# Attention with keys on the partitions: maxima from one product, exponents not transposed, the causal mask as a product

## What is computed

```python
sc = einsum('bgpqd,bgnd->bgpqn', qb, k_cmp)            # compressed keys
p_c = softmax(where(valid_c, sc, NEG_INF)); o_c = p_c @ v_cmp
ss = einsum('bgpqd,bgqnld->bgpqnl', qb, k_sel)         # selected blocks
p_s = softmax(where(key_pos <= t_pos, ss, NEG_INF)); o_s = p_s @ v_sel
sw = einsum('bgpqd,bgkd->bgpqk', qb, kwb)              # window
p_w = softmax(where(valid_w, sw, NEG_INF)); o_w = p_w @ vwb
o = gate0 * o_c + gate1 * o_s + gate2 * o_w
```

## Time and profile before

| | us |
|---|---|
| median of 3 runs (lowest to highest) | 2381.58 (2381.36 to 2381.64) |
| the profiled execution | 2382.09 |
| its span | 2380.3 |
| PE busy in it | 2370.0 |
| DVE busy | 1332.7 |
| ACT busy | 899.4 |
| POOL busy | 310.5 |

### The profile page before, as it was taken

The page is one execution under the profiler, slowest core; times in us unless marked ns, Lnnn a source line. Parts: engine busy times, 40 slices in busy tenths (PEclk is TensorE's granted clock), DMA queues, the critical chain, the costliest instruction groups (busy, mean ns, idle before and its releaser), DMA issues.

```text
span 2380.3 us, 33586 instructions
## 1 busy us (share of the span) xinstructions
PE 2370.0 (100%) x11768; PEld 2002.1 (84%) x11768; DVE 1332.7 (56%) x2199; ACT 899.4 (38%) x1376; POOL 310.5 (13%) x305
## 2 busy tenths in 40 slices
PE   9999999999999999999999999999999999999998
PEld 7899988888888888888888888888889998888887
DVE  8667765344465764443586644446756676534444
ACT  6267833222233432222233322223426773322223
POOL 2211140000040120000033000003420114000003
PEclk9999999999999999999999999999999999999999
DMA  4710023232233232322233223233370002223232
GB/s 165 224 46 2 2 69 108 88 101 93 99 105 106 89 106 91 103 97 97 97 99 106 97 91 104 89 106 105 121 208 27 2 2 89 97 89 106 89 105 89
DMA packets 64616, 220.58 MB, mean 93 GB/s; under 512 B 7680, under 2 KB 7808, under 8 KB 64512
## 3 DMA queue, kind: packets, MB, share of 16 engines
q1 hardware_dynamic: 58320, 208.59, 26.3%
q0 software_dynamic: 5184, 8.40, 1.6%
q10 hardware_dynamic: 1008, 2.21, 0.3%
HBM read 208.68 MB, written 2.10 MB: 89 GB/s over the span
## 4 chain that ended last, share of the span: by engine, by line
PE 99%; DVE 0%; DMA 0%; ACT 0%; SPq 0%; issue 0%; DVEq 0%
PE bank L1516 95%; PE bank L1796 3%; DMA x<-x_in 0%; PE bank L1826 0%; DVE branch L1281 0%; DVE big L1509 0%; SPq L434 0%; DVE rden L1276 0%; ACT L588 0%; DVE w_lo L939 0%; DVE rden L1278 0%; ACT w_hi L572 0%; PE bank L1700 0%; ACT xs_hi L581 0%; ACT xg L907 0%
## 5 line engine op out<-in xcount | busy, mean ns | idle before, releaser
L1516 PE MATMUL bank<-xs_hi,w_hi 128*128 128x512 f32 (+1 forms) x1808 | 708.9, 392 | 1.1 <-DVE xs_lo L947 0.5
L1516 PE MATMUL bank<-xs_lo,w_hi 128*128 128x512 f32 (+1 forms) x1808 | 703.3, 389 | 0.0
L1516 PE MATMUL bank<-xs_hi,w_lo 128*128 128x512 f32 x1792 | 697.3, 389 | 0.0
L939 DVE TENSOR_TENSOR w_lo<-raw,w_hi 128x1024 fp32r<-128x1024 f32 x369 | 469.7, 1276 | 230.7 <-ACT w_hi L572 226.3
L572 ACT ACTIVATE w_hi<-raw 128x1024 fp32r<-128x1024 f32 x372 | 390.8, 1051 | 432.6 <-PE bank L1516 231.7
L1516 PEld LDWEIGHTS bank<-xs_hi,w_hi 128*128 128x128 f32 (+1 forms) x1808 | 339.0, 188 | 74.4 <-DVE xs_lo L947 1.5
L1516 PEld LDWEIGHTS bank<-xs_lo,w_hi 128*128 128x128 f32 (+1 forms) x1808 | 338.4, 187 | 71.0 <-issue 1.0
L1516 PEld LDWEIGHTS bank<-xs_hi,w_lo 128*128 128x128 f32 x1792 | 336.4, 188 | 70.0
L1516 PE MATMUL bank<-hid_hi,w_hi 128*128 128x512 f32 x720 | 280.5, 390 | 0.0
L1516 PE MATMUL bank<-hid_lo,w_hi 128*128 128x512 f32 x720 | 280.1, 389 | 0.0
L1516 PE MATMUL bank<-hid_hi,w_lo 128*128 128x512 f32 x720 | 280.1, 389 | 0.0
(11 more groups left out here) (212 smaller groups left out, 2719.8 us busy)
## 6 DMA issues: line engine op xcount, KB each, us to landing
raw<-stream SPq DMA_DIRECT2D x371, 512.0 KB, 3.2
w_f<-stream SPq DMA_DIRECT2D x18, 512.0 KB, 3.5
hid_hi<-mix_hi POOLq DMA_DIRECT2D x32, 128.0 KB, 3.7
hid_lo<-mix_hi POOLq DMA_DIRECT2D x32, 128.0 KB, 3.1
out<-big SPq DMA_DIRECT2D x8, 256.0 KB, 2.9
x<-x_in ACTq DMA_DIRECT2D x4, 256.0 KB, 6.8
x<-x_in SPq DMA_DIRECT2D x4, 256.0 KB, 7.5
big<-consts SPq DMA_DIRECT2D x1, 664.0 KB, 11.0
```

Of the source, the lines that this page charges most:

```text
L939: nc.vector.tensor_tensor(w_lo[:, slot, :], raw[:, k, :], f32(w_hi[:, slot, :]), ALU.subtract).then_inc(w_lo_ready, counted(b))
L1516: return nc.tensor.matmul(out_, w, v, start=start, stop=stop)
```

## The change

Packs and their score products stay, but only to find the maxima: one product a unit, with `key_hi` alone, and `maximum` writes the masked scores into a throwaway tile (`unused`, bf16) and the negated maxima of an item into `nmax` (8 columns of 4 x 64: column 0 of a head for the selected branch, 32 for the window). When the packs of an item are through, PE transposes `nmax` (`turn_rows`, four transposes with 64 stationary columns) into rows, and ACT copies them into the upper half of `qa`, whose lower half holds the high parts of the four heads' queries once more (`queries_again`, two instructions an item). POOL overwrites in `key_lo` one row of the upper half for each branch with ones and the other with zeros (`key_pad`, four memsets of one partition and 2048 elements).

The scores are then computed again with the keys on the partitions, in *blocks*: 128 keys against 4 heads x 128 queries, 512 columns. A block is `key_hi` times the queries plus `key_lo` times `qa`, which adds the low part of the keys and subtracts the maxima; on the diagonal the mask is added as the product of the identity with `behind` (bf16). ACT exponentiates from PSUM straight into `pt`, from where the products with the values take it as it is: the transposes and their copies are gone, except for the compressed scores. An item has 1 + 2(t + 1) blocks, 24 a group, 96 a layer. The packs and row transposes are *turns*, 120 a layer, numbered from 0; step s has the turns that `step_of` gives it, block s and the products of block s - 3. Turn k waits for the maxima (or the row copy) of turn k - 2. The first group's items now run t = 0, 1, 2, 3, the others as before.

```diff
 def t_of(i):
-    return TT - 1 - i % TT
+    return i if i < TT else TT - 1 - i % TT
...
+def turns_of_layer():
+    out = []
+    for i in range(ITEMS):
+        mine = [("pack", p) for p in range(NPACKS) if PACKS[p][0] == i]
+        out += mine[:2] + ([("rows", i - 1)] if i else []) + mine[2:]
+    return out + [("rows", ITEMS - 1)]
...
+HEAD = 4
+def step_of(k):
+    if k < HEAD:
+        return k // 2 - 2
+    return max((k - HEAD) // 2, (4 * (k - 13)) // 5)
...
+                for row in range(2):
+                    for br in range(2):
+                        if row + br:
+                            gp.wait_ge(key_pad, 4 * a + 2 * row + br)
+                        gp.memset(f32(key_lo[DH + 32 * row:DH + 32 * row + 1, br, :, :].rearrange("p g t -> p (g t)")),
+                                  1.0 if row == br else 0.0).then_inc(key_pad, 1)
...
+                def rows(i):
+                    queries_again(a, i)
+                    act.wait_ge(rows_turned, i0 + i + 1)
+                    nc.scalar.activation(qa[DH:P, i % 3, :], bank[score_bank(l0, TURN_OF_ROWS[i])][0:DH, :], ACT.Copy
+                                         ).then_inc(rows_ready, 1)
+                def block(b):
+                    w = P if BLOCKS[b][1] < 0 else S
+                    act.wait_ge(block_ready, n0 + b + 1)
+                    wait_past(act, pv_done, n0 + b - 3)
+                    nc.scalar.activation(pt[:, b % 4, 0:w], bank[turn_bank(l0, b)][:, 0:w],
+                                         ACT.Copy if BLOCKS[b][1] < 0 else ACT.Exp).then_inc(pt_ready, 1)
...
-                        for j in range(n):
-                            nc.vector.tensor_tensor_reduce(
-                                out=prob[:, p % 4, bass.ts(j, w)], in0=bank[score_bank(l0, p)][:, bass.ts(j, w)],
-                                in1=causal_b[:, S - w:S], scale=-1.0, scalar=-NEG, op0=ALU.add, op1=ALU.min,
-                                accum_out=nmax[:, p % 4, j:j + 1]).then_inc(max_ready, 1)
+                        for k, (br, j) in enumerate(units(p)):
+                            last = nc.vector.tensor_tensor_reduce(
+                                out=unused[:, p % 2, bass.ts(k, w)], in0=src[:, bass.ts(k, w)], in1=causal_b[:, S - w:S], scale=-1.0,
+                                scalar=-NEG, op0=ALU.add, op1=ALU.min, accum_out=nmax[:, i % 2, j, 32 * br:32 * br + 1])
+                        last.then_inc(max_ready, 1)
...
                         for k, (br, j) in enumerate(units(p)):
-                            q = q_home[g][:, j, bass.ts(t, P)]
-                            mm(dst[:, bass.ts(k, w)], q, key_hi[:, br, g, 0:w], True, False)
-                            last = mm(dst[:, bass.ts(k, w)], q, key_lo[:, br, g, 0:w], False, True)
+                            last = mm(dst[:, bass.ts(k, w)], q_home[g][:, j, bass.ts(t, P)], key_hi[:, br, g, 0:w],
+                                      True, True)
...
-                def turn(p):
-                    wait_copied(pe, a, p - 2)
...
+                def turn_rows(i):
+                    pe.wait_ge(max_ready, p0 + max(p for p in range(NPACKS) if PACKS[p][0] == i) + 1)
+                    for j in range(4):
+                        last = nc.tensor.transpose(bank[score_bank(l0, TURN_OF_ROWS[i])][0:DH, bass.ts(j, P)],
+                                                   nmax[:, i % 2, j, :], ident[:, :])
+                    last.then_inc(rows_turned, 1)
...
+                def block(b):
...
+                    wait_past(pe, pt_ready, n0 + b - 1)
...
+                        mm(dst[:, :].rearrange("p (j q) -> p j q", j=4), key_hi[:, br, g, bass.ts(kb, P)],
+                           q_home[g][:, :, bass.ts(t, P)], True, False)
+                        last = mm(dst[:, :], key_lo[:, br, g, bass.ts(kb, P)], qa[:, i % 3, :], False, kb < t)
+                        if kb == t:
+                            pe.wait_ge(behind_ready, 1)
+                            last = mm(dst[:, :].rearrange("p (j q) -> p j q", j=4), ident_b[:, :],
+                                      behind[:, :].unsqueeze(1).broadcast_to([P, 4, P]), False, True)
```

More of the change, by code:

```diff
@@ L1740, in turn_gates @@
                     last.then_inc(gate_turned, 1)
-                steps, rest = attention(l, a)
+                turns, rest = attention(l, a)
                 def first_packs():
@@ L1827, in turn_out @@
                     last.then_inc(osum_t, 1)
-                def steps(lo, hi):
-                    for s in range(lo, hi):
-                        if s < NPACKS:
-                            scores(s)
-                        if 0 <= s - TURN < NPACKS:
-                            turn(s - TURN)
                 def out_part(k, lo, hi):
@@ L1852, in rest @@
                 def rest():
-                    for s in range(LATE, NPACKS + SUM_T):
-                        steps(s, s + 1)
-                        if s == LATE:
-                            products(LATE - 1 - MULT)
-                        if 0 <= s - MULT < NPACKS:
-                            products(s - MULT)
+                    for s in range(NBLOCKS + SUM_T):
+                        turns(s)
+                        if s < NBLOCKS:
+                            block(s)
+                        if 0 <= s - LAG < NBLOCKS:
+                            products(s - LAG)
                         for i in items_at(s, LAST_W, SUM_T):
@@ L1871, in rest @@
                     out_part(2, 2, MT)
-                return steps, rest
+                return turns, rest
             def sgu(l):
```

276 lines of the change are left out of this document (150 added, 126 removed).

## The result

The changed kernel takes 2392.81 us in the median (its profiled execution 2392.72, with a span of 2390.8), the kernel before 2381.61. The ratio is 1.0046, with a 95% interval of 1.0036 to 1.0057. The prediction was 2378.2 us in a range of 2370 to 2391, with 0.19 for slower. The time is above that range, and slower is what came. One of its six executions, at a mean granted clock of 0.698, took 4213.44 us and is left out of the ratio; the other five lie between 2391.59 and 2393.82.

What follows compares the result with a forecast made beforehand. TensorE (PE) was taken as the bound. Per layer, -5.2 us of PE work, +3.7 of start waits and -0.2 for waits already there gave -1.7, both layers -3.4: 2378.2 us, range 2370 to 2391.

Steps and rivals of the forecast that it cites:

- What bounds the kernel: Whole kernel: TensorE bounds it, busy 2370.0 of 2380.3 us, so the change matters through PE's queue in two attention layers.
- What leaves the queue: PE's queue per group of four items: second score products 4.6 us, transposes 8.8, switches 0.2; together 13.6 us.
- What comes in: PE's queue per group: block products, masks, row transposes and the products behind them add 12.3 us.
- the mask: Eight diagonal blocks a group: one bf16 product of 512 columns each at 0.22 us, 1.8 us, up to 2.2.
- the row transposes: Four per item, 16 a group, with 64 stationary columns: 0.07 us each, 1.1 us, upper bound 1.8.
- the block products: 20 blocks a group, two 512-column products each: 40 x 0.227 = 9.1 us, plus 0.35 behind row transposes.
- No waits in a steady group: Groups after the start: PE never idle, no turn finds its maxima missing; period 39.9 us instead of 41.2.
- The start: Steps 0 to 12 of each layer: PE waits for DVE's maxima, losing about 3.7 us, bounds 1.5 and 6.
- What costs nothing: POOL's four memsets, about 7.6 us, fit its idle time; ACT loses more copies than it gets; DMAs and SP unmoved.
- (c): Rival, chance 0.18: DVE holds PE up all along, in 18 later two-turn steps a layer, 0.4 us each: 2392.
- (b): Rival, chance 0.17: new PE products at the dear end of their prices, 0.2 to 0.6 us a group: 2384 to 2387.
- (a): Rival, chance 0.20: the start-up wait does not come because DVE keeps up: 2373, down to 2370.

Runs made afterwards that it cites:

- rows_half: Changed kernel with only two of the four transposes of each row turn (that part of the computation left out): 2388.45 us, ratio 1.0026.
- bank_free_early: Changed kernel with turns that reuse the compressed-score bank waiting for VectorE's first operation on it, not the third: 2390.93 us, ratio 1.0038.
- Max_first: Changed kernel with the maxima of turns 4, 6 and 7 ahead of VectorE's scaling of the last value tile: 2391.04 us, ratio 1.0037.
- act_values: Changed kernel with ScalarE instead of VectorE scaling the last two of four value tiles: 2388.55 us, ratio 1.0030.
- rows_later: Changed kernel with the last row turn (item 15) at step 88 instead of step 84: 2389.86 us, ratio 1.0032.
- mask_on_pool: Changed kernel with the diagonal causal mask as a GpSimd multiplication on the exponents instead of a PE product: 2382.26 us, ratio 1.0004.
- no_mask: Changed kernel without the mask products on the 64 diagonal blocks (that part of the computation missing): 2380.95 us, ratio 0.9997.
- three_edits: Changed kernel with mask on GpSimd, two value tiles scaled by ScalarE and last row turn at step 88: 2375.81 us, ratio 0.9976.
- four_edits: Changed kernel with mask on GpSimd, two value tiles on ScalarE, last row turn at step 88 and earlier score-bank release: 2374.51 us, ratio 0.9970.

## Point by point: what held and what did not

**What bounds the kernel.** Held: PE is busy 100% of the span before and 99% after, and every edit that took work from PE's queue in a steady group moved the time.

**What leaves the queue.** Held. By start-to-start times of one group in both traces 4.7 us of second products and 9.1 of transposes are gone, and 0.3 in the score products that stay; forecast were 4.6, 8.8 and 0.2.

**What comes in.** This is the first step that failed: 12.3 us a group was the forecast, and it is 13.4, with 0.6 more at the instructions that stay (waits and switches). Of its four prices,
- the mask held: 1.82 us for eight (0.228 each), forecast 1.8;
- the row transposes failed. They follow one another every 0.11 us; I had priced them at 0.07 because the weight load of 64 columns is short. It is short, 119 ns against the 188 of the earlier trace rows, but the next transpose does not come sooner. A row turn of four takes 0.36 us and not 0.28 (212.51 to 212.87), and the product behind it 0.32 and not 0.23 (212.87 to 213.19), as I had it. That is 0.3 to 0.35 us a group, and rows_half confirms the 0.108;
- the block products are 10.1 us for 40, not 9.1 + 0.35. 13 of the 20 first ones start their successor after 0.23 us, but 7 after 0.314, four behind row transposes and three behind the narrow mask of a compressed pack. I had counted the four only. The second ones stand mostly at 0.232 to 0.239, not 0.227, and behind one of them PE comes 0.21 us later than that.

The timeline of PE at a row turn in after:

```profile
212.51 0.60 PE L1847 MATMUL bank<-ident,nmax 128*64 128x128 f32 x4
212.87 0.48 PE L1575 MATMUL bank<-mix_lo,hid_hi 128*128 128x512 f32 x1
213.19 0.40 PE L1575 MATMUL bank<-qa,hid_lo 128*128 128x512 f32 x1
```

The group of weight loads of the row transposes in the first layer (count | busy us, mean ns):

```profile
L1847 PEld LDWEIGHTS bank<-ident,nmax 128*64 128x64 f32 x64 | 7.1, 119 | 2.3 <-issue 1.3 <-DVE prob_c L1324 0.6
```

The prediction set the rule of the Trainium skill (TensorE: Matmul & The Clock Gate, section LDWEIGHTS) beside this, by which the group would have been another 0.2 us shorter. The load did get shorter, by 69 ns for 64 columns, though it is 119 ns and not the rule's 53, and the measurement decides. But neither the rule nor my slope says when the next transpose starts.

**No waits in a steady group.** Failed: "PE idle nowhere in it" was the forecast, and after has, beyond the pace from start to start, 0.34 us at the row turn of 207.29 shown with bank_free_early, 0.28 and 0.21 us at two other places. Before had one stop of 0.36. That row turn is the one of item 6, the very one to which the prediction gave the smallest slack, 0.15 us. I had followed the queue to see whether maxima are late. I had not looked at which operation of DVE gives a bank back: the row turn waits for the third of three, and bank_free_early gave back 0.26 us a group by waiting for the first. Together with the prices of the point above, 41.0 us instead of 39.9: 4.4 us a layer, 8.8 of the 14.6 us by which the prediction missed. This is the step that turned a small gain into a loss.

**The start.** The mechanism held and its sum was near, a little too small. The layer costs 4.7 us; four groups at -0.2 and 1.27 at the end leave 4.1 to 4.2 us for the start, where 3.7 less the 0.2 of before was forecast, in bounds of 1.5 to 6. Counted directly, PE's products of the second layer between 1804.6 and 1834.6 us stand 4.1 us over the pace of a steady group, from start to start. The sign was not quite met: of "3 to 4 us" idle for maxima the profile shows 2.4 a layer, and 0.6 for prob_c and ScalarE's rows. The first stall was mis-sized, 1.95 us and not 1.1. DVE was 0.4 us earlier than I said (144.91 for the maxima of turn 4, forecast 145.3), but PE was at the end of the values at 142.02 and not at the 143.46 of the earlier trace rows, 1.4 us earlier. I had taken this moment from the trace of before, although the score turns among the values lose their second products and their transposes too, which is 1.0 us of it; by the other 0.4 this execution was ahead already at its first compressed product. What PE saves ahead of a wait only makes the wait longer. Max_first shows that the stall is not a matter of one order, act_values that it is DVE's sum of work.

**The row turn of item 15.** Missed altogether. I followed the steps 0 to 12 and 24 to 48, and not the last ones, where the turn table puts the last score turn and the row turn that needs its maxima into one step. 1.12 us of idle time, 1.27 with the switch, twice; rows_later gave it back.

**The clock.** Not foreseen: 1.5 to 1.8 us in the first layer. PE had been busy without a break, stood for 1.95 us, and 1.2 us after it went on its clock fell from the higher level to the lower one, for most of the stretch from 146 to 153 us. See below for what is not settled.

**What costs nothing.** Held. GpSimd's four memsets take 7.39 us (7.6 forecast) and end well before the value copies, with 7.31 us to spare:

```profile
104.18 7.39 POOL L562 MEMSET hid_lo<- 1x2048 f32 x4 [2.72 <-DMA hid_lo<-mix_hi]
118.88 1.22 POOL L568 COPY vbd_all<-vcf 32x64 f32<-32x64 f32 x2 [7.31 <-ACT vcf L783]
```

ScalarE is not a bound: it has 23.6 us of work in 40, and PE waits 0.3 us for it in the whole execution of after.

**The rivals.** The time is that of (c), 2392, by coincidence; its mechanism did not come: the waits do not lie in the 18 later steps with two turns. They stand at the start, at the end, and in a steady group at the bank release and two other places, about 0.8 us a group in all. Of (b), dear prices, a part came true (a group at 40.7 without the avoidable wait), and with the end and the clock on top it comes to 2392. (a) is refuted by the 1.95 us. The chances had (b) and (c) as alternatives; they came partly together, with a third loss in neither.

In short, the medians miss by 14.6 us and the profiled executions by 14.0 (the span grew by 10.6 where it should have lost 3.4): 8.8 in the period of the groups (some 40% of it in waits, the rest prices), 2.5 at the row turn of item 15, 1.3 at the starts, 1.5 by the clock, less the 0.4 by which this execution was early. The small rest is rounding.

## What to carry to other kernels

Where another engine hands over buffers, recount the moment at which the bounding engine arrives with the savings of the change in it, and follow its queue to the very last step; a gain ahead of a fixed hand-over turns into a wait. For small matrix products take the start-to-start time of the nearest whole operation, since a shorter weight load does not say that the next one starts sooner. And a mask that costs TensorE 0.23 us a tile is a good thing to give to an idle engine, when its three steps of lead are there already; look then at what that engine shares with the others.

## What the runs showed of the hardware

**TensorE's clock after a stall.** The granted clock fell to 1.2 GHz for a few microseconds soon behind the first stall of a layer in some executions and not in others: in after in the first layer only, in rows_half and mask_on_pool in both, in no_mask in the second, in rows_later and bank_free_early in none. The stall was 1.94 to 1.95 us in all of these but rows_half, where it was 2.16. In max_first, act_values and three_edits, whose longest stall there is 1.0 us, 0.63 and 0.63, it did not fall; in four_edits, with 0.63 us, it did once. So longer stalls went with it more often (in six of the twelve layers against one of eight), but what decides is open. It may be why some medians moved by 1 to 2 us more or less than twice what their second layer did. The executions on record fit that: in no_mask and rows_half those with the lowest mean clock took longest, and in mask_on_pool eight with 0.998 or 0.999 took 2381.83 to 2382.54 us, those with 0.997 and 0.996 took 2383.24 and 2384.53.

**GpSimd's own time.** Its multiplication of 128x512 with the broadcast bf16 triangle took 1.15 to 1.31 us, mean 1.18, and not the 1.59 that the expectation took from an operation on two f32 tiles of this shape in before. VectorE operations that read two SBUF operands and begin while it runs last until it is through: 0.91 us instead of 0.17, 1.04 instead of 0.42, and a pair of them 0.6 us more. Where the VectorE operation begins first, it keeps its time.

**Row transposes.** Stationary operands of 64 columns load in 119 ns instead of 188, and the transposes still come every 0.11 us, like those of 128 columns in the earlier trace rows.

Not tried: spreading the pairs of score turns at item 3 (0.31 us of idle time at 163.68 in after, and in every variant of it), which is left in four_edits too (0.30 us at 160.76).
